# One stage for the norm of the attention output, its projection and the norm behind it, in a decoder layer on one Trainium2 core

## What is computed

```python
def merge_heads(o_fox, o_nsa, g, w_out):
    o = jnp.concatenate([rmsnorm(o_fox, g[:FOX_W]), rmsnorm(o_nsa, g[FOX_W:])], axis=-1)
    return o @ w_out                       # 1024 x 1024
...
x = x + merge_heads(...)
...
gu = rmsnorm(x, g_norm) @ w_gu             # 1024 x 5632
g, u = gu[..., :D_FF], gu[..., D_FF:]      # D_FF = 2816
g_ext = jnp.concatenate([hist.astype(g.dtype), g], axis=1)
for i in range(CONV_W):                    # CONV_W = 3
    gc = gc + conv_w[i] * g_ext[:, i:i + T]
y = (jax.nn.silu(gc) * u) @ w_down         # 2816 x 1024
return x + y, g_ext[:, -(CONV_W - 1):]
...
y_prompt = rmsnorm(xp, final_norm_g)
```

## Time and profile before

| | us |
|---|---|
| median of 3 runs (2313.81 to 2320.35) | 2315.79 |
| the profiled execution, its own time | 2314.83 |
| its span in the trace | 2313.2 |
| TensorE matmul busy | 1928.1 (83%) |
| VectorE busy | 1000.5 (43%) |
| ScalarE busy | 751.3 (32%) |
| GpSimd busy | 540.7 (23%) |

### The profile page before, as it was taken

The page is one execution under the profiler, slowest core; times in us unless marked ns, Lnnn a source line. Parts: engine busy times, 40 slices in busy tenths (PEclk is TensorE's granted clock), DMA queues, the critical chain, the costliest instruction groups (busy, mean ns, idle before and its releaser), DMA issues. The chain is left out here.

```text
span 2313.2 us, 32369 instructions
## 1 busy us (share of the span) xinstructions
PE 1928.1 (83%) x11816; PEld 1686.3 (73%) x11816; DVE 1000.5 (43%) x1876; ACT 751.3 (32%) x1454; POOL 540.7 (23%) x636
## 2 busy tenths in 40 slices
PE   3996879996565488999999569589999999969996
PEld 3885877785443277888888558389999999946774
DVE  2334223113232245777777531423333333345997
ACT  2223002112221015777777520322222222222452
POOL 4310012125242511222221000022222222133552
PEclk9897899997897658999999779689999999989999
DMA  5532636224855572222220032311111111054334
GB/s 131 96 71 84 200 127 229 85 100 140 274 183 184 136 148 69 56 56 60 65 56 1 12 133 79 102 53 54 36 54 36 54 36 54 18 197 163 131 125 148
DMA packets 176335, 233.48 MB, mean 101 GB/s; under 512 B 44252, under 2 KB 120469, under 8 KB 176087
## 3 DMA queue, kind: packets, MB, share of 16 engines
q1 hardware_dynamic: 149674, 152.52, 21.7%
q0 software_dynamic: 26544, 79.45, 12.2%
HBM read 196.95 MB, written 40.18 MB: 103 GB/s over the span
## 5 line engine op out<-in xcount | busy, mean ns | idle before, releaser
L118 PE MATMUL gate_acc<-h_T_hi,w_gate_split_hi 128*128 128x352 f32 x528 | 172.4, 326 | 7.7 <-POOL w_gate_split_lo L2533 7.7
L2296 DVE TENSOR_TENSOR pa_probs_T_lo<-pa_t,pa_probs_T_hi 128x512 fp32r<-128x512 f32 (+3 forms) x288 | 147.5, 533 | 64.6 <-ACT pa_probs_T_hi L2237 63.6
L118 PE MATMUL up_acc<-h_T_hi,w_up_split_hi 128*128 128x352 f32 x528 | 170.3, 323 | 0.0
L120 PE MATMUL gate_acc<-h_T_hi,w_gate_split_lo 128*128 128x352 f32 x528 | 170.2, 322 | 0.0
L119 PE MATMUL gate_acc<-h_T_lo,w_gate_split_hi 128*128 128x352 f32 x528 | 170.1, 322 | 0.0
L119 PE MATMUL up_acc<-h_T_lo,w_up_split_hi 128*128 128x352 f32 x528 | 169.2, 321 | 0.0
L120 PE MATMUL up_acc<-h_T_hi,w_up_split_lo 128*128 128x352 f32 x528 | 169.1, 320 | 0.0
L2237 ACT ACTIVATE pa_probs_T_hi<-pa_t 128x512 fp32r<-128x512 f32 (+3 forms) x288 | 131.9, 473 | 90.7 <-PE pa_t L2162 87.3
L2162 PE MATMUL pa_t<-ident,pa_scores 128*128 128x128 f32 x816 | 138.7, 276 | 17.5 <-DVE pa_probs_T_lo L2296 17.5
L2222 ACT ACTIVATE pa_scores<-pa_scores,pa_neg_max 128x128 f32<-128x128 f32 (+1 forms) x192 | 143.3, 746 | 30.4 <-DVE pa_neg_max L2260 26.2
L118 PE MATMUL y_acc<-w_down_split_hi,act_split_hi 128*128 128x512 f32 x308 | 126.8, 412 | 29.8 <-DVE act_split_lo L2796 25.7
(11 more groups left out here) (424 smaller groups left out, 4849.2 us busy)
## 6 DMA issues: line engine op xcount, KB each, us to landing
w_down_raw<-in_w_down SPq DMA_DIRECT2D x60, 512.0 KB, 4.6
fox_k_pages<-in_cache_fox_kv SPq DMA_DIRECT2D x64, 256.0 KB, 8.5
w_rows<-in_cache_fox_kv POOLq DMA_DIRECT2D x64, 256.0 KB, 6.0
w_gate<-in_w_gu SPq DMA_DIRECT2D x22, 512.0 KB, 3.7
w_up<-in_w_gu SPq DMA_DIRECT2D x22, 512.0 KB, 3.8
sel_pages<-in_cache_nsa_kv POOLq DMA_DIRECT2D x64, 128.0 KB, 7.6
pa_k_fox<-scratch_kf_d POOLq DMA_DIRECT2D x32, 256.0 KB
w_rows<-in_w_in SPq DMA_DIRECT2D x3, 2048.0 KB, 14.6
```

The costliest lines, as they stand in the source:

```text
L118: pe.matmul(out, a[0][at], b[0][bt], start=start, stop=False)
L120: return pe.matmul(out, a[1][at], b[0][bt], start=False, stop=stop)
L2296: dve.tensor_tensor(lo, PT[n % 2][:, 0:m * P].rearrange("p (m n) -> p m n", n=P), hi, ALU.subtract).then_inc(s_cd, 1)
```

## The change

The two norms, the projection and their transposes become one stage, `output_and_norm`. For step 0 to 10 the order on PE is: transposes of attention tile `step`, product of tile `step - 1`, transposes of the normed sum of tile `step - 2`. The sum x1 no longer comes back from DRAM for its norm (it is still stored, since `down` adds to it). All of `w_out` has room at once; its even row blocks are loaded by SP and rested by POOL, the odd ones loaded by POOL and rested by DVE. The weights of gate_up's block 0 are loaded, rounded and rested in the new stage (`GateWeights`), into the room of attention tiles that have been turned. gate_up begins with the gate product of block 0; the tables are turned on PE between it and the up product. In `down` the product that needs only a sum of activations comes first, its first chunk of weights is loaded at gate_up's end, x is loaded back in four loads of 1 MB behind chunks 2 to 5, the sample rows' products stand beside the second and third product, and chunks are two steps (the last of a product one).

```diff
-def output_projection(c, oT):
+def output_and_norm(c, oT, wo, gate):
...
         @block.sync
         def _(sp):
-            for k in range(KD):
-                if k >= 2:
-                    sp.wait_ge(s_lo, k - 1)
-                sp.dma_start(w[:, k % 2, :], d["w_out"][0, k * P:(k + 1) * P, :]).then_inc(s_w[k], 16)
+            sp.dma_start(g1[:, :], d["out_norm_g"][0:1, :].to_broadcast([P, D])).then_inc(s_g1, 16)
+            for k in range(0, KD, 2):
+                sp.dma_start(raw[:, k, :], d["w_out"][0, k * P:(k + 1) * P, :]).then_inc(s_w[k], 16)
+            sp.dma_start(x_s[0:NS, :], d["os_d"]).then_inc(s_xs, 16)
             for t, rows in enumerate(ROWS):
                 if t >= 3:
                     sp.wait_ge(s_st[t % 3], 16 * (t // 3))
+                    sp.wait_ge(s_xn2, t - 2)
                 src = d["x_prompt"][0, t * P:(t + 1) * P, :] if t < NT else d["x_sample"].rearrange("b q n -> (b q) n")
                 sp.dma_start(x[t % 3][0:rows, :], src).then_inc(s_x[t % 3], 16)
+                if t == 0:
+                    sp.dma_start(g2[:, :], d["norm2_g"][0:1, :].to_broadcast([P, D])).then_inc(s_g2, 16)
+            sp.wait_ge(s_t1, NT)
+            gate.load(sp, 0)
 
...
+            def turn_o(t):
+                rows = ROWS[t]
+                pe.wait_ge(s_xn1, t + 1)
+                if t:
+                    pe.wait_ge(s_l1, t)
+                for k in range(KD):
+                    ins = pe.transpose(tp1[:, k * P:k * P + rows], o_rows(t, k * P, (k + 1) * P), c.ident[0:rows, 0:rows])
+                ins.then_inc(s_t1, 1)
+
+            def product(t):
+                rows = ROWS[t]
+                pe.wait_ge(s_l1, t + 1)
                 if t >= 2:
                     pe.wait_ge(s_v, t - 1)
                 for k in range(KD):
-                    if t == 0:
-                        pe.wait_ge(s_lo, k + 1)
+                    if t == 0 and k % 2 == 0:
+                        pe.wait_ge(s_wp, k // 2 + 1)
+                    if t == 0 and k % 2 == 1:
+                        pe.wait_ge(s_wd, k // 2 + 1)
                     for a in range(2):
-                        ins = split_products(pe, acc[t % 2][0:rows, a * 512:(a + 1) * 512], oT, ws, np.s_[:, k, t * P:t * P + rows],
+                        ins = split_products(pe, acc[t % 2][0:rows, a * 512:(a + 1) * 512], oT, wo, np.s_[:, k, t * P:t * P + rows],
                                              np.s_[:, k, a * 512:(a + 1) * 512], k == 0, k == KD - 1)
                 ins.then_inc(s_pe, 1)
...
+            for step in range(NR + 2):
+                if step < NR:
+                    turn_o(step)
+                if 1 <= step <= NR:
+                    product(step - 1)
+                if step >= 2:
+                    turn_x(step - 2)
...
+            for t in range(2):
+                squares_o(t)
+                root_o(t)
+            round_w(0)
+            copy_o(0)
+            for k in range(1, KD):
+                round_w(k)
+            for step in range(1, NR + 3):
+                if step < NR:
+                    copy_o(step)
+                if 0 <= step - 3 < NR:
+                    copy_x(step - 3)
+                if 0 <= step - 2 < NR:
+                    squares_x(step - 2)
+                    root_x(step - 2)
+                if step + 1 < NR:
+                    squares_o(step + 1)
+                    root_o(step + 1)
+                if step == NR:
+                    gate.round(act, 0)
...
+            scale_o(0)
+            scale_o(1)
+            rest_o(0)
+            for k in range(1, KD, 2):
+                dve.wait_ge(s_wh, k + 1)
+                dve.tensor_tensor(wo[1][:, k, :], raw[:, k, :], wo[0][:, k, :], ALU.subtract).then_inc(s_wd, 1)
+            for step in range(1, NR + 3):
+                if 0 <= step - 2 < NR:
+                    add(step - 2)
+                if step < NR:
+                    rest_o(step)
+                if 0 <= step - 3 < NR:
+                    rest_x(step - 3)
+                if 0 <= step - 2 < NR:
+                    scale_x(step - 2)
+                if step + 1 < NR:
+                    scale_o(step + 1)
...
         def _(pool):
+            for k in range(1, KD, 2):
+                pool.dma_start(raw[:, k, :], d["w_out"][0, k * P:(k + 1) * P, :]).then_inc(s_w[k], 16)
+            for k in range(0, KD, 2):
+                pool.wait_ge(s_wh, k + 1)
+                pool.tensor_tensor(wo[1][:, k, :], raw[:, k, :], wo[0][:, k, :], ALU.subtract).then_inc(s_wp, 1)
             for t, rows in enumerate(ROWS):
                 pool.wait_ge(s_v, t + 1)
                 pool.dma_start(d["x1_d"][t * P:t * P + rows, :], x[t % 3][0:rows, :]).then_inc(s_st[t % 3], 16)
+                if t == NT - 1:
+                    gate.rest(pool, 0)
...
+    def load(self, sp, f):
+        for side in range(2):
+            sp.dma_start(self.w[side][:, :, :], self.d[:, :, ds(f * P + side * FF, P)]).then_inc(self.s_w[side], 16)
+
+    def round(self, act, f):
+        for side in range(2):
+            act.wait_ge(self.s_w[side], 16 * f + 16)
+            act.activation(self.ws[side][0][:, :, :], self.w[side][:, :, :], ACT.Copy).then_inc(self.s_hi[side], 1)
+
+    def rest(self, pool, f):
+        for side in range(2):
+            pool.wait_ge(self.s_hi[side], f + 1)
+            pool.tensor_tensor(self.ws[side][1][:, :, :], self.w[side][:, :, :], self.ws[side][0][:, :, :], ALU.subtract)\
+                .then_inc(self.s_lo[side], 1)
...
-            for side in range(2):
-                sp.sem_inc(s_lo[side], 1)
-            with sp.Fori(0, NF) as f:
+            with sp.Fori(1, NF) as f:
                 for side in range(2):
-                    sp.wait_ge(s_lo[side], f + 1)
-                    sp.dma_start(w[side][:, :, :], w_gu[:, :, ds(f * P + side * FF, P)]).then_inc(s_w[side], 16)
+                    sp.wait_ge(s_lo[side], f)
+                    sp.dma_start(w[side][:, :, :], gate.d[:, :, ds(f * P + side * FF, P)]).then_inc(s_w[side], 16)
+            sp.dma_start(first[:, :, :], d["w_down"][0, 0:2 * P, 0:D // 2].rearrange("(f p) n -> p f n", p=P)).then_inc(s_first, 16)
...
+                pe.wait_ge(s_ld, 48)
+                pe.transpose(E_[0][:, 0, 0:4 * NF], cw_rows[0:4 * NF, :], c.ident[0:4 * NF, 0:4 * NF]).then_inc(s_et, 1)
...
+            products(0, 0, G_, s_g, s_gc)
+            tables()
+            products(0, 1, U_, s_u, s_a)
+            products(1, 0, G_, s_g, s_gc)
+            products(1, 1, U_, s_u, s_a)
+            with pe.Fori(1, NF // 2) as i:
                 for b in range(2):
...
+                    products(2 * i + b, 0, G_, s_g, s_gc)
+                    products(2 * i + b, 1, U_, s_u, s_a)
...
-            act.wait_ge(s_z, 2)
-            act.wait_ge(s_ec, NE + 1)
             act.sem_inc(s_gc, 1)
...
+            act.wait_ge(s_z, 2)
+            act.wait_ge(s_ec, NE + 1)
...
+            columns(0, 0)
+            rounded(1)
+            columns(1, 1)
+            with act.Fori(1, NF // 2) as i:
+                for b in range(2):
+                    rounded(2 * i + b)
+                    columns(2 * i + b, b)
...
 PRODUCTS = [
+    ((((1, 0), 1), ((1, 1), 1)), (((0, 0), 1),), (((1, 0), 1), ((1, 1), -1))),
     ((((0, 0), 1),), (((0, 1), 1), ((1, 1), -1)), (((0, 1), 1), ((1, 1), 1))),
     ((((1, 1), 1),), (((1, 0), 1), ((0, 0), -1)), (((0, 0), 1), ((1, 0), 1))),
     ((((0, 0), 1), ((1, 1), 1)), (((0, 0), 1), ((1, 1), 1)), (((0, 0), 1), ((1, 1), 1))),
-    ((((1, 0), 1), ((1, 1), 1)), (((0, 0), 1),), (((1, 0), 1), ((1, 1), -1))),
     ((((1, 0), 1), ((0, 0), -1)), (((0, 0), 1), ((0, 1), 1)), (((1, 1), 1),)),
     ((((0, 0), 1), ((0, 1), 1)), (((1, 1), 1),), (((0, 0), -1), ((0, 1), 1))),
     ((((0, 1), 1), ((1, 1), -1)), (((1, 0), 1), ((1, 1), 1)), (((0, 0), 1),)),
 ]
...
-    CHUNKS = [(0, 1)] + [(a, 2) for a in range(1, HF, 2)]
+    CHUNKS = [(a, min(2, HF - a)) for a in range(0, HF, 2)]
+    SAMPLES = {1: 1, 2: 0}
...
-                    if at >= RB:
+                    if at == 0:
+                        continue
+                    if at > RB:
...
                     for i, ((fh, ch), sign) in enumerate(PRODUCTS[p][1]):
                         sp.dma_start(raw[at % RB][:, i, 0:m, :],
                                      w_d[:, fh * HF + k0:fh * HF + k0 + m, ch * HW:(ch + 1) * HW]).then_inc(s_r[at % RB], 16)
-                    if at == 3:
-                        for t in range(0, NT, 4):
-                            sp.dma_start(y[:, t:t + 4, :], d["x1_d"][t * P:(t + 4) * P, :].rearrange("(t p) n -> p t n", p=P))\
-                              .then_inc(s_x, 16)
-                        sp.dma_start(y[0:NS, NT, :], d["x1_d"][T:TT, :]).then_inc(s_x, 16)
+                    if 2 <= at < 6:
+                        t = (at * 2) % NT
+                        sp.dma_start(y[:, t:t + 2, :], d["x1_d"][t * P:(t + 2) * P, :].rearrange("(t p) n -> p t n", p=P))\
+                          .then_inc(s_x, 16)
```

(23 more changed lines are left out.)

279 lines of the change are left out of this document (184 added, 95 removed).

## The result

The changed kernel takes 2231.7 us, median of 4 runs (2228.1 to 2237.8), against 2316.0 before (4 runs, 2313.8 to 2320.4): ratio 0.9636, 95% interval 0.9611 to 0.9662. Forecast were 2238, 2222 to 2260.

A forecast was written before the change was run, and what follows sets the result against it. TensorE's idle and half-clock time between attention and gate_up, and down's DMA order, were taken as the bound. 69.6 - 4.1 + 12.4 = 77.9 us off 2314.83 gives 2236.9, plus 1.0 for the median: 2238, range 2222 to 2260.

The forecast's parts named there:

- Until the first product: New stage: first projection matmul 13 us behind the first square, at about 1320.5, with loads at 268 GB/s.
- the first product: New stage: matmuls bind, not weights; 4.2 us at half clock, end at 1333.4, add 26 us behind the first square.
- Steps: New stage: seven steps of 13.0 us, a 10.99 us product and two times eight transposes at full clock; 91.0 us.
- the first rival: New stage: the clock falls in every step, eight times 3.5 us, 28 us in all, giving 2266; chance 0.12.
- The stage: Joined norms and projection, up to the first gate matmul: that matmul comes 69.6 us earlier.
- gate_up: Tables' transposes between two products cost 3.1 us and the next gate product is late by about 1: 4.1 us lost.
- The gate_up loop behind its first block: gate_up after block 0: claimed to stay as it is, with no gain or loss counted.
- down's start: Start of down: POOL needs only act_T and can begin with DVE at 2034.8, 3.5 us gained.
- down's stalls: Down after its start: 6.29 us stall, 1.6 of fallen clock and 4.0 of add waits go, against a 3.0 loss.
- The two waits of 2.0 for a bank's add: Down: both TensorE waits go because even chunks issue the load a step earlier; 4.0 us gained.
- The cost of heavy neighbours: Down: two products needing sums of both operands now adjoin, DVE being nearly full; 3.0 us lost, bounds 0 and 5.
- Sum: Whole kernel: 69.6 - 4.1 + 12.4 = 77.9 us less, forecast 2238.

The follow-up runs named there:

- down_as_before: Changed kernel with all of the old down (product order, first chunk of one block, x in two loads, no early load): 2242.7 us.
- down_sooner: Changed kernel with down's first two sums of act_T made in gate_up and no wait for the convolution's stores at its end: 2230.3 us.
- turns_times_five: Changed kernel with attention tiles 2 to 8 each turned five times over, 48 transposes between two products in place of 16: 2254.4 us, one run.
- idle_each_step: Changed kernel with a TensorE pause of about 5 us ahead of products 1 to 8, waiting on four GpSimd additions: 2286.0 us, one run.
- norm1_apart: Changed kernel with all nine tiles of the first norm turned ahead of the first product, second norm staying in the steps: 2254.9 us.
- x_two_loads: Changed kernel with x in down loaded as before, two loads of four tiles and two small ones behind the fourth weight chunk: 2230.1 us.
- old_order_new_loads: Changed kernel with the old down order and no early load, but even chunks and x in four spread loads; first add awaits sample rows: 2243.1 us.
- after: The changed kernel itself, against the kernel before: 2231.7 us, ratio 0.9636.

## Why the prediction was right, and where its terms were off

- **Until the first product** (+13.0; measured +12.2) and **the first product** (+25.9; +24.6). The loads ran at 337 GB/s, not 268, and the clock was up after 1.3 us of matmuls, not 4.2. That was luck of the execution: in `down_as_before` and `down_sooner`, whose program is the same up to there, it took 4.2 and 4.5 us, and the add came at +25.6 and +25.7, as forecast.
- **Steps** (13.0; 12.86) at a clock of 1.00: right, and the reason too. The doubt was whether transposes hold the clock. Those of 128 x 128 do here, three times as many as well, so the first rival fell. The Trainium skill, "TensorE: Matmul & The Clock Gate", Part 4: PE-mode transpose, says that a transpose doesn't count as PE busy in the same way. For 128 x 128 and a clock that is already up, `turns_times_five` (1.00) against `idle_each_step` (0.83) speaks against that; the fall behind the 40 small ones agrees with it.
- **The stage** (69.6; 71.7). The runs divide it: second norm 27.2, first norm 22.5, first gate weights 6.8, the tables ahead of them on SP and ACT 5.6, and early `w_out` 9.1 (the first product's add came 62.9 us behind the first square before, 53.8 in `norm1_apart`). That is 71.2, and 0.5 is left over. The last two come from comparing traces, not from a run of their own. Of the 2.1 us over the forecast, 1.3 lie ahead of the first add and 0.8 behind it.
- **gate_up** (4.1 lost; 0.9 won). The mis-sized term. The tables cost 3.3 us between the products, and the next gate product was late by 0.4, near the 3.1 and 1 of the sum, without a fall of the clock; but I had "The gate_up loop behind its first block" stay as it is, and it didn't: 4.8 us went with ACT's table loads.
- **down's start** (3.5; 3.6 by `down_as_before`, 2.8 against the kernel before). Right, or 0.7 too much.
- **down's stalls** (8.9 net; 9.9 by `down_as_before`, 12.5 against the kernel before). Size near, and in part by luck. I gave the stall's end to fewer bytes and to x being spread together: with even chunks, fewer bytes were enough without the spreading (`x_two_loads`), and the estimate from `old_order_new_loads` has the spreading enough without fewer bytes. The two waits of 2.0 for a bank's add are gone, as said. The cost of heavy neighbours (3.0) isn't there: the two products together take 68.8 us, and 68.9 when they stand apart. The old down took 253.0 us behind the new stages and 255.6 behind the old ones; all of that lies in its first product (45.0 and 47.6 us), where the stall was 4.7 and 6.3. Why the stall was shorter stays open.
- **Sum** (77.9; 84.3 between medians, 87.0 between the two traces from the first square). Of the 9.1 missed by the traces, 2.1 are the stage, 5.0 gate_up, the rest down, its 1.0 lost behind the last matmul taken off. The medians lie 2.7 us nearer to the forecast than the traces.

## What to carry to other kernels

Where TensorE waits for a chain over other engines, put the chain's next tile behind the product of the last: nine tiles' turns cost 1.0 us each inside the steps and some 3 to 4 apart. Where a change brings two cures for one stall, take each out alone, and look in the trace whether the wait that is left is the old one: in `old_order_new_loads` it came from the edit. Give a small late load its own semaphore, or everything that waits for the large ones waits for it. Look in the loops for loads of an activation table at the head: one turn written out ahead of the loop removed twenty.

## What the runs showed of the hardware

- Transposes of 128 x 128 float32, 48 in a row (5.4 us), left the granted clock at 1.00; 5.0 us of waiting brought half speed for the next 5.3 us. Eight of them and 40 of 32 x 32 (3.6 us, no wait) were followed by half speed for 3.4 us.
- The same program differs from one execution to the next in when the clock moves: it rose 1.3, 4.2 and 4.5 us into the first product (`after`, `down_as_before`, `down_sooner`); a wait of 2.38 us in down had a fall behind it in the changed kernel (0.50 from 2095.2 to 2098.7), one of 2.37 in `x_two_loads` none.
- Two small stores issued by GpSimd held the meeting of the engines back by 4.1 us with nothing waiting for them; issued by SyncE, 1.3.
- A rest of 128 x 512 on VectorE takes 0.68 us, and 1.75 beside a sum on GpSimd. The Trainium skill, "SBUF — State Buffer", section "SBUF: two separate sides", has the two engines share a port pair that one holds for a whole instruction; these rows agree with it.
- The same program ahead of the first square took 1307 to 1317 us from one execution to the next.
